# Two transforms of the last Hyena filter, and one weight split, placed later in the opening of a two-layer diffusion backbone

## The reference, cut to what matters

```python
def reference(x, c, ctx, c_ctx, ada_w, ada_b, norm_g, w_out, ev_w_in, ...):
    h_lat, h_ctx = x, ctx                                  # 256 latent and 256 context tokens, D = 2048
    for i in range(DEPTH):                                 # 2 layers
        sh_l, sc_l, g_l = jnp.split((jax.nn.silu(c) @ ada_w[i] + ada_b[i])[:, None, :], 3, axis=-1)
        sh_c, sc_c, g_c = jnp.split(jax.nn.silu(c_ctx) @ ada_w[i] + ada_b[i], 3, axis=-1)
        u_lat = _rmsnorm(h_lat, norm_g[i]) * (1.0 + sc_l) + sh_l
        u_ctx = _rmsnorm(h_ctx, norm_g[i]) * (1.0 + sc_c) + sh_c
        ...                                                # layer 0: window attention || Hyena; layer 1: attention || MLA
        h_lat = h_lat + g_l * (o_lat @ w_out[i])

def _hyena_filters(L, w1, b1, f1, w2, b2, f2, w3):         # a small MLP of the position makes the filters
    ...
    h = (h @ w3.astype(F32)).reshape(L, HYENA_ORDER, 2, B_WIDTH)
    return h * jnp.exp(-t[:, None] * deltas[None, :])[:, None, None, :]

def _long_conv(u, h):
    k = jnp.concatenate([h[:, 0], jnp.zeros_like(h[:1, 0]), h[:0:-1, 1]], axis=0)
    k = k / jnp.sum(jnp.abs(k), axis=0, keepdims=True)
    kf = jnp.fft.rfft(k, n=2 * L, axis=0)
    ...
```

## Time and profile before

| | before |
|---|---|
| median of 3 runs | 1486.72 us (1485.7 to 1490.14) |
| profiled execution | 1485.43 us, span of the core 1483.6 us |
| PE busy | 1434.4 us, 97% |
| DVE, ACT, POOL busy | 968.7, 541.2, 261.9 us |
| PE busy in 93 to 142 us | 46.27 of 49 us |

### The profile page before, as it was taken

The page is one execution under the profiler, slowest core; times in us unless marked ns, Lnnn a source line. Parts: engine busy times, 40 slices in busy tenths (PEclk is TensorE's granted clock), DMA queues, the critical chain, the costliest instruction groups (busy, mean ns, idle before and its releaser), DMA issues.

```text
span 1483.6 us, 18434 instructions
## 1 busy us (share of the span) xinstructions
PE 1434.4 (97%) x7415; PEld 1145.8 (77%) x7415; DVE 968.7 (65%) x1176; ACT 541.2 (36%) x764; POOL 261.9 (18%) x292
## 2 busy tenths in 40 slices
PE   5999999999999999999999899999999889999998
PEld 1336887888887878778888688888888768788998
DVE  3385998889997877786786645447445544455543
ACT  2554212222222433443323412126356554455432
POOL 1000333322332000000002143432010421000000
PEclk9999999999999999999999999999999999999999
DMA  9998654565555554455466766634234331323563
GB/s 349 404 362 349 184 186 153 159 222 156 193 165 164 187 172 147 125 175 175 160 212 220 252 229 201 230 113 155 91 127 153 125 135 60 111 87 114 190 221 129
DMA packets 65173, 272.24 MB, mean 184 GB/s; under 512 B 6784, under 2 KB 17216, under 8 KB 45376
## 3 DMA queue, kind: packets, MB, share of 16 engines
q1 hardware_dynamic: 44912, 193.45, 37.2%
q0 software_dynamic: 20176, 77.61, 16.4%
HBM read 256.36 MB, written 14.68 MB: 183 GB/s over the span
## 4 chain that ended last, share of the span: by engine, by line
PE 90%; DMA 5%; DVE 2%; POOL 2%; ACT 1%; issue 1%; ACTq 0%; DVEq 0%; POOLq 0%
PE banks L1036 20%; PE banks L1037 20%; PE banks L1040 20%; DMA ada_ring<-in_ada_first 2%; PE banks L1991 2%; PE banks L1992 2%; PE banks L1997 2%; PE banks L2152 2%; PE banks L1218 2%; PE banks L1205 2%; PE banks L2026 1%; PE banks L1301 1%; DMA hybias<-in_hy_bias 1%; PE banks L2139 1%; PE banks L1269 1%; PE banks L551 1%
## 5 line engine op out<-in xcount | busy, mean ns | idle before, releaser
L1036 PE MATMUL banks<-xh,wh 128*128 128x512 f32 (+1 forms) x1536 | 538.3, 364 | 0.1
L1037 PE MATMUL banks<-xl,wh 128*128 128x512 f32 (+1 forms) x1536 | 525.3, 355 | 0.0
L998 DVE TENSOR_TENSOR wl<-raw,wh 128x2048 fp32r<-128x2048 f32 (+1 forms) x125 | 283.1, 2265 | 101.3 <-ACT wh L992 101.3
L1036 PEld LDWEIGHTS banks<-xh,wh 128*128 128x128 f32 x1536 | 290.1, 189 | 49.6 <-issue 9.3
L1037 PEld LDWEIGHTS banks<-xl,wh 128*128 128x128 f32 x1536 | 290.3, 189 | 43.3 <-issue 3.8
L992 ACT ACTIVATE wh<-raw 128x2048 fp32r<-128x2048 f32 (+1 forms) x125 | 236.5, 1892 | 238.2 <-PE banks L1040 171.3
L1040 PE MATMUL banks<-xh,wl 128*128 128x512 f32 (+1 forms) x1536 | 310.9, 355 | 0.0
L1040 PEld LDWEIGHTS banks<-xh,wl 128*128 128x128 f32 x1536 | 257.0, 189 | 40.5
L409 POOL DMA_DIRECT2D ada_w<-in_ada_rest x128 | 69.0, 540 | 554.6 <-DVE ada_acc L398 381.6
L386 DVE SCALAR_TENSOR_TENSOR ada_acc<-ada_w,cond,ada_acc 128x1024 f32<-128x1024 f32 x120 | 159.8, 1332 | 5.2 <-DMA ada_w<-in_ada_rest 3.1
L398 DVE SCALAR_TENSOR_TENSOR ada_acc<-ada_w,cond,ada_acc 128x1024 f32<-128x1024 f32 x90 | 125.3, 1393 | 0.0
(11 more groups left out here) (313 smaller groups left out, 1714.2 us busy)
## 6 DMA issues: line engine op xcount, KB each, us to landing
ada_w<-in_ada_rest POOLq DMA_DIRECT2D x128, 512.0 KB, 4.1
raw<-in_ev_tiles SPq DMA_DIRECT2D x52, 1024.0 KB, 6.6
ada_ring<-in_ada_first SPq DMA_DIRECT2D x32, 1024.0 KB, 12.6
raw<-in_out_tiles SPq DMA_DIRECT2D x32, 1024.0 KB, 5.1
raw<-in_od_wide SPq DMA_DIRECT2D x16, 1024.0 KB, 4.8
raw<-in_od_gates SPq DMA_DIRECT2D x16, 1024.0 KB, 4.9
hT<-in_hT POOLq DMA_DIRECT2D x4, 1024.0 KB, 12.3
spectra<-kstage POOLq DMA_DIRECT2D x4, 1024.0 KB, 10.5
```

What stands on the lines that cost most here:

```text
L998: nc.vector.tensor_tensor(b.wl[:, t % 2, 0:width], b.raw[:, t % 2, 0:width], b.wh[:, t % 2, 0:width].bitcast(F32), ALU.subtract).then_inc( ...
L1036: nc.tensor.matmul(out, wh[:, k, :], b.xh[:, seg, k, :], start=(k == 0), stop=False)
L1037: nc.tensor.matmul(out, wh[:, k, :], b.xl[:, seg, k, :], start=False, stop=False)
```

## The change

The table of stages is now one for each filter. Filters 0 to 2 keep theirs. Filter 3, which begins in tick 16, has its stage 2 in tick 20 instead of 19 and its stage 3 in tick 22 instead of 20. DVE's low split of tile 0 stands in tick 23 instead of 21. Nothing is added or removed. The title given with the change speaks of two and four ticks; from `FILTER_TICK` 16 the ticks are 16, 18, 20, 22 after and 16, 18, 19, 20 before.

```diff
 FILTER_TICK = (1, 6, 11, 16)
-STAGE_TICK = (0, 2, 3, 4)
+STAGE_TICK = ((0, 2, 3, 4),) * 3 + ((0, 2, 4, 6),)
 SQUARE_TICK = 7
 SPLIT_HIGH = {18: 0, 26: 1}
-SPLIT_LOW = {21: 0, 26: 1}
+SPLIT_LOW = {23: 0, 26: 1}
...
     for f, first in enumerate(FILTER_TICK):
-        if tick - first in STAGE_TICK:
-            return f, STAGE_TICK.index(tick - first)
+        if tick - first in STAGE_TICK[f]:
+            return f, STAGE_TICK[f].index(tick - first)
```

## The result

The changed kernel took 1494.07 us (median of 6 runs, 1493.57 to 1494.57), the kernel before 1487.55 us (6 runs, 1485.7 to 1491.33). The ratio is 1.0036, 95% interval 1.0024 to 1.0049, so the change makes the kernel some 5.4 us slower (3.6 to 7.3). The forecast was 1494.4 us, and the medians are 6.5 us apart. The profiled execution took 1494.57 us (span 1492.8).

A forecast was written before the change was run, and what follows sets the result against it. PE was taken to bound the kernel (90% of the chain that ended last). Lost cover 3.77, write waits 1.8 and 0.3, and clock 1.8 summed to +7.7 us: 1494.4 us beside the median of 1486.72, range 1490.3 to 1497.3.

The forecast's parts named there:

- The cover: PE, ticks 19 to 28: stage 2's 5.04 us leave a wait for `arow`; less 0.57 and 0.70, 3.77 us lost.
- The waits given back: PE up to tick 28: waits of 0.57 us for `wl` and 0.70 us for ring piece 27 go.
- the 0.81 us at tick 24: PE's wait for `arow` of tick 23: stays, because ACT's copy follows PE's products as before.
- The clock: PE, ticks 20 and 21: the new 5.70 us wait lowers the granted clock, costing 1.8 us (bounds 0 and 3).
- The row in layer 1: PE in layer 1: after a 5.44 us wait the granted clock was 0.52; taken as nearest in length.
- the wait of 2.96 us: PE's wait up to 49.59 us, after which the clock stayed 1.00; cited against a fall of the clock.
- The wait for the last write: Last spectrum's write, taken as 11.1 us, makes PE wait 1.8 us at tick 28 and some 0.3 us at tile 1.
- the 112 to 114.5 us: POOL: sign that the last L531, issuing the last spectrum's write, comes between these times.
- the 6.3 us: POOL: the last spectrum's write is issued this much later, at 111.95 instead of 105.64.
- rival 3: Tick 28: no wait for the write, which lands within 9.3 us; +5.6 us, 1492.3. Chance 0.15.
- The second fall of the clock: Tick 28: the 1.8 us wait also lowers PE's clock, about 1.6 us more; +9.3, 1496.0. Chance 0.15.
- Rival 5: Tick 20: third spectrum's write lands before 91 us, so no cover exists; 1.3 us less, 1485.4. Chance 0.03.

The follow-up runs named there:

- e6: Changed kernel with 6 extra matmuls behind tick 19's products, filling PE's wait; ratio 1.0043 to the kernel before.
- e1: Changed kernel with filter 3's stage 2 back in tick 19, only stage 3 later (tick 22); ratio 1.0010 to the kernel before.
- e5: Changed kernel with tile 0's high split on ACT moved behind `arow` and normalization of tick 19; ratio 1.0001 to the kernel before.
- e4: Kernel before with tile 0's high split on ACT moved behind `arow` and normalization of tick 19; ratio 0.9998 to the kernel before.
- e7: Changed kernel run again with no edit; ratio 1.0041 to the kernel before.
- e2: Changed kernel with filter 3's stage 3 in tick 21 instead of 22, stage 2 still in tick 20; ratio 1.0026 to the kernel before.
- e3: Changed kernel with 12 extra matmuls behind tick 19's products; ratio 1.0059 to the kernel before.

## Why the prediction was right, and where not

**The cover: right.** 3.77 us were forecast for the lost cover less the waits for `wl` and piece 27. The stretch of e6, free of the clock and less the write's waits, is +3.78. That close a match is chance: tick 19 to 20 took 6.32 us in e6 and 6.60 before, and e6's ticks 28 to 29 are 0.53 us longer than the changed kernel's for a wait listed as 0.30. e1 and e5 show the mechanism from both sides: with stage 2 back in the wait, or with the wait gone, the loss goes.

**The waits given back: right.** Those of 0.57 and 0.70 us are gone from the changed kernel, and the 0.81 us at tick 24 stayed. The wait ahead of tick 20 was 5.21 and 5.45 us, not 5.70. That is the third write, ahead of everything moved, which took 9.98 us in the changed profile where it had taken 10.32.

**The clock: right, a little small.** 1.8 us were forecast; the direct measure is 2.25 and 1.92. The row in layer 1 was a better neighbour than the wait of 2.96 us, after which the clock had stayed up. That second row was one draw of several: at the same place (the wait ends at 49 to 54 us) the clock fell in the changed kernel's profile, with a wait of 2.54 us, and in those of e1 (3.31), e4 (2.55), e5 (2.55) and e7 (3.27), but not in those of e2 (2.54), e3 (3.18) and e6 (2.54).

The Trainium skill's page TensorE: Matmul & The Clock Gate (Part 1: The HAM clock gate) lets an idle PE fall back to half rate. Both traces of the changed kernel agree, with a granted clock of 0.50 around 100 us.

**The wait for the last write: wrong, 2.1 us too much.** The step that failed is the term "I take the 11.1 us that this same write took". The issue came at 115.89, outside the 112 to 114.5 us that were given as a sign; less the opening's 1.82 us it is 114.07, inside them, so the 6.3 us and the clock were right. But the write took 8.5 and 8.6 us, so rival 3 is what happened. I reasoned that ring pieces 28 to 30 would stand beside the write as 26 and 27 had, and took the write's duration from there. Pieces did stand beside it, but two things differ. The write's first packets moved some 3.5 us behind the issue and not 4.4. And for a microsecond the ring's queue moved little, and the write got most of the engines where it had had half (DMA queues of the changed kernel in 122 to 123 us):

```profile
q0 software_dynamic: 42, 0.34, 81.1%
q1 hardware_dynamic: 32, 0.07, 16.8%
```

Ahead of the write the ring had run empty: pieces are issued only as PE is done with others, PE had stood still and then done stage 2, and the engines' share was 0.23 in 108 to 112 us. Pieces issued beside the write landed after 6.9 to 9.9 us, and after 11.3 to 13.6 in the kernel before. The traces order the write's length by its place: 11.1, 10.6, 10.8 and 10.1 us where it is issued at 105.6 to 109.3 (before, e4, e5, e1), 9.1 at 112.9 (e2), 8.5 to 9.9 at 115.9 to 116.7. That the ring's smaller backlog makes the difference fits all this, but no run changes the backlog alone. Nor is it known why the same write takes 8.5 and 8.6 us in the changed kernel and 9.7 and 9.9 in e3 and e6. In all four some 1.03 of its 1.05 MB had moved by 8 us behind the issue; in e3 and e6 the last 0.02 MB came later.

**The sum.** In the stretch: 3.77 - 0.34 (the shorter first wait, 6.26 us from tick 19 to 20 and not 6.60) + 2.25 = 5.68; measured 5.62. The forecast's 7.7 us is 2.1 too many, which is the two waits of 1.8 and 0.3 us that the write's 11.1 us had given. That the median came out within 0.4 us of 1494.4 is partly luck: the ratio says 5.4 us, and the median of before fell 0.8 us above the one I added to.

**The other rivals.** The second fall of the clock didn't come; even 1.75 us of wait in e5 brought none. Rival 5 needed the wait to vanish. e5 makes it vanish in another way, and the loss does go (+0.01%); the gain of 1.3 us that the rival gave did not come, since the write's waits took 2.04 us.

## What to carry to other kernels

Before work is moved out of a stretch in which an engine would otherwise wait, ask what releases the engine there: if it is something that the work doesn't delay or hasten, all of the work is paid for at its new place, and the now empty wait can cost the clock on top (here 3.8 us, and some 2 us on PE for the clock, for 5 us of matmuls that had cost nothing). Conversely the wait's cause can be removed, and then the place matters less. A transfer need not keep its duration when its issue moves: this one had 11.1 us in one place and 8.5 in another. Take its range from all its neighbours, not the value it had.

## What had not been expected of the hardware

The last spectrum's write of 1 MB took 8.5 to 11.1 us from issue to landing in nine traces, in which only the order and amount of other work differ. Its first packets moved 4.4 us behind the issue in the kernel before and 3.5 us in the changed one: of the software queue, none in the 2 us behind the issue at 115.89, then 0.13 MB in the next 2.

And an empty wait of some 5 us cost more than its own length: for some 5 us behind its end the instructions took up to 1.8 times as long (1.94 us for 1.07, 1.86 for 1.02), 1.92 and 2.25 us in all in two traces. A shorter wait was not safe either: every trace has a wait of 2.5 to 3.3 us that ends at 49 to 54 us, and in five of the nine the granted clock fell to 0.50 within it or just behind it. The one in the changed kernel's profile set it back 1.64 us.
